# A 2-layer hybrid decoder step: tile products in two PSUM banks, reordered copies, gate work and output pieces, and a VectorE transposition in place of a third product

## The reference

```python
lmat = jnp.where(strict, jnp.einsum('nbhid,nbhjd->nbhij', kb, kc) * decay, 0.0)
rhs = jnp.concatenate([kb * jnp.exp(gc)[..., None], vc * bc[..., None]], axis=-1)
sol = lax.linalg.triangular_solve(eye + lmat, rhs, left_side=True, lower=True, unit_diagonal=True)
...
def step(S, xs):
    v_new = u_i - jnp.einsum('bhck,bhkv->bhcv', w_i, S)
    o = (jnp.einsum('bhck,bhkv->bhcv', q_i * jnp.exp(g_i)[..., None], S)
         + jnp.einsum('bhij,bhjv->bhiv', qk_i, v_new))
    S = S * jnp.exp(g_last)[..., None, None] + jnp.einsum('bhck,bhcv->bhkv', k_dec, v_new)
    return S, o
```

## Time and profile before

| | |
|---|---|
| median of 3 runs | 3659.48 us (3659.13 to 3660.59) |
| the profiled execution | 3668.19 us, its span 3666.5 us |
| PE busy | 3337.3 us, 91% of the span |
| DVE / ACT / POOL busy | 1865.3 / 827.3 / 847.5 us |
| granted TensorE clock, whole span | 0.922 |

### The profile page before, as it was taken

One profiled execution on the slowest core, in us unless ns is written; L12 is line 12 of the kernel. 1 busy time (PEld: TensorE's weight loads), 2 busy tenths in 40 slices (PEclk: granted clock), 3 DMA queues, 4 the chain that ended last, 5 costly groups with the idle time before them and its releaser, 6 DMA issues.

```text
span 3666.5 us, 74612 instructions
## 1 busy us (share of the span) xinstructions
PE 3337.3 (91%) x32699; PEld 3143.0 (86%) x32699; DVE 1865.3 (51%) x4027; ACT 827.3 (23%) x1897; POOL 847.5 (23%) x776
## 2 busy tenths in 40 slices
PE   6889898989898898988999999995699899999998
PEld 5878797978787787877999999994499799999997
DVE  5445555455554454556876777635512433423334
ACT  3334333324242332333010111002200300000001
POOL 2102020202020111201333333332323133333331
PEclk8879898989898897989999999996699899999999
DMA  2111111111111111110112222226611011111111
GB/s 90 55 42 50 59 44 59 47 49 52 48 54 44 55 55 49 48 42 30 49 61 84 72 84 78 71 65 217 180 41 47 29 47 47 47 47 47 47 48 62
DMA packets 111348, 223.82 MB, mean 61 GB/s; under 512 B 24880, under 2 KB 59184, under 8 KB 110000
## 3 DMA queue, kind: packets, MB, share of 16 engines
q1 hardware_dynamic: 82400, 177.66, 15.2%
q10 hardware_dynamic: 28624, 41.38, 3.5%
HBM read 177.86 MB, written 41.14 MB: 60 GB/s over the span
## 4 chain that ended last, share of the span: by engine, by line
PE 85%; DVE 8%; ACT 3%; issue 2%; DMA 2%; SPq 1%; POOL 0%; POOLq 0%; DVEq 0%; ACTq 0%
PE ps L218 31%; PE ps L626 15%; PE ps L1360 14%; PE ps L702 5%; PE ps L660 4%; PE ps L677 1%; PE ps L234 1%; PE ps L671 1%; PE ps L653 1%; PE ps L638 1%; DVE x L1172 1%; PE ps L727 1%; PE ps L789 1%; PE ps L295 1%; DVE dwork L1282 1%
## 5 line engine op out<-in xcount | busy, mean ns | idle before, releaser
L218 PE MATMUL ps<-hhi,whi 128*128 128x344 f32 x2424 | 779.1, 321 | 19.1 <-DVE hlo L1829 15.3
L218 PE MATMUL ps<-hhi,wlo 128*128 128x344 f32 x2424 | 776.3, 320 | 0.0
L218 PE MATMUL ps<-hlo,whi 128*128 128x344 f32 x2424 | 775.6, 320 | 0.0
L2099 POOL TENSOR_TENSOR wtick<-wtick 128x1 f32<-128x1 f32 x213 | 46.5, 218 | 2619.4 <-PE ps L218 811.9
L2102 POOL TENSOR_TENSOR wlo<-wraw,whi 128x1024 fp32r<-128x1024 f32 x213 | 531.1, 2493 | 17.1
L218 PEld LDWEIGHTS ps<-hhi,whi 128*128 128x128 f32 x2424 | 457.6, 189 | 21.8 <-issue 17.0
L218 PEld LDWEIGHTS ps<-hhi,wlo 128*128 128x128 f32 x2424 | 457.3, 189 | 0.0
L218 PEld LDWEIGHTS ps<-hlo,whi 128*128 128x128 f32 x2424 | 456.7, 188 | 0.1
L626 PE MATMUL ps<-hhi,whi 128*128 128x344 f32 x1152 | 395.6, 343 | 5.1 <-DVE olo L1092 2.7
L626 PE MATMUL ps<-hhi,wlo 128*128 128x344 f32 x1152 | 376.2, 327 | 0.0
L626 PE MATMUL ps<-hlo,whi 128*128 128x344 f32 x1152 | 376.1, 326 | 0.0
(11 more groups left out here) (366 smaller groups left out, 5544.1 us busy)
## 6 DMA issues: line engine op xcount, KB each, us to landing
wraw<-in_w SPq DMA_DIRECT2D x213, 512.0 KB, 3.3
dwork<-keep_rows SPq DMA_DIRECT2D x64, 256.0 KB, 3.7
tab<-keep_tab SPq DMA_DIRECT2D x8, 1088.0 KB, 6.4
S<-in_sin ACTq DMA_DIRECT2D x16, 512.0 KB, 3.7
drw<-keep_del SPq DMA_DIRECT2D x32, 256.0 KB, 3.3
out_sout<-S ACTq DMA_DIRECT2D x16, 512.0 KB, 2.8
keep_u<-hs SPq DMA_DIRECT2D x8, 580.0 KB, 3.2
uu<-keep_u SPq DMA_DIRECT2D x8, 580.0 KB, 7.7
```

What stands on the lines that cost most here:

```text
L218: ins = nc.tensor.matmul(out, w, r[:, kt, blk(n)], start=k == 0, stop=k == 3 * KT - 1)
L2099: G.tensor_tensor(wtick[:, 1:2], wtick[:, 0:1], wtick[:, 0:1], ALU.add)
```

## The change

- `LEV` goes: P products of all four matrices go to bank `LP` = 0 (columns 32j), T and Y to bank `LT` = 1. The tile order is now j outside, zone inside: four consecutive tile matmuls have four zones and one bank. Banks 2 and 3 join `aside` in the level stage (`free`).
- The T product of levels 1 to 4 goes. DVE adds Y alone (L1291) and then transposes the sum in 32x32 blocks into the T half (L1293). T5 stays on PE.
- The copy `NTc` moves from ACT to DVE (L1136), behind NT. `T5` moves from DVE to ACT (L915). `YD` is done after `Y5` (zones 2, 3) and after P6 (zones 0, 1), not ahead of it. P6 waits for `T5` alone; `vn` waits for `YD` also.
- `gate_mul` moves from slot 5 to 7, `gate_lo` from 7 to 10, `gate_hi` from 6 to 9. In the next i's first projection the gate sum moves behind the fourth half block, and its ACT and DVE parts behind those of the chain.
- Output pieces move to other slots (quad 0: 7 to 6; quad 1: 2, 7 to 5, 9; quad 2: 7, 8 to 6, 9; quad 3: 7 to 5).

```diff
@@ -556,16 +556,18 @@
         SLOTS = 12
-        COL_P, COL_T, COL_Y = 0, Z, 2 * Z
         DENSE = (0, 1, 2, 3, 5, 6, 7)
-        LEV, CB = (0, 1, 2, 3), 4
+        LP, LT, CB = 0, 1, 4
...
-        def across(col, w, r=slice(0, P)):
-            return ps[r, 0:4, col:col + w]
-        PIECE_SLOTS = ((0, 1, 2, 3, 4, 7, 8, 9), (0, 2, 3, 4, 6, 7), (0, 3, 4, 7, 8), (0, 3, 4, 6, 7))
+        def of_p(r=slice(0, P)):
+            return ps[r, LP, 0:4 * Z].rearrange("p (j n) -> p j n", n=Z)
+
+        def of_ty(r=slice(0, P)):
+            return ps[r, LT, 0:8 * Z].rearrange("p (j n) -> p j n", n=2 * Z)
+        PIECE_SLOTS = ((0, 1, 2, 3, 4, 6, 8, 9), (0, 3, 4, 5, 6, 9), (0, 3, 4, 6, 9), (0, 3, 4, 5, 6))
...
@@ -593,8 +595,8 @@
             held = {}
-            dense = 0
-            free = {5: 0, 6: 0, 7: 0}
+            dense = base = 0
+            free = {2: 0, 3: 0, 5: 0, 6: 0, 7: 0}
...
@@ -606,7 +608,10 @@
                 dense += 1
-                return use(DENSE[(dense - 1) % 7], who, name)
+                b = DENSE[(dense - 1) % 7]
+                if b in free:
+                    free[b] = base + dense / 100
+                return use(b, who, name)
...
@@ -653,12 +658,21 @@
-            def tiles(col, lhsT, rhs):
-                for d in range(4):
-                    for j in range(4):
-                        r = zone((j + d) % 4)
-                        ins = nc.tensor.matmul(ps[r, LEV[j], col:col + Z], lhsT(r, j), rhs(r, j), start=True, stop=True)
+            def tiles(out, lhsT, rhs):
+                for j in range(4):
+                    for z in range(4):
+                        r = zone(z)
+                        ins = nc.tensor.matmul(out(r, j), lhsT(r, j), rhs(r, j), start=True, stop=True)
                 return ins
+
+            def to_p(r, j):
+                return ps[r, LP, Z * j:Z * j + Z]
+
+            def to_t(r, j):
+                return ps[r, LT, 2 * Z * j:2 * Z * j + Z]
+
+            def to_y(r, j):
+                return ps[r, LT, 2 * Z * j + Z:2 * Z * j + 2 * Z]
...
@@ -672,6 +686,7 @@
                     p.after("DVE", g + "Y6")
+                    p.after("ACT", g + "YD")
...
@@ -757,30 +772,26 @@
                     for h in range(2):
-                        jj = (j + h) % 4
                         up, low = zone(2 * h), zone(2 * h + 1)
-                        ins = nc.tensor.matmul(ps[low, LEV[jj], COL_P:COL_P + Z], DEC[q % 2][up, jj, low], W[up, jj, 0:Z], start=True, stop=True)
+                        ins = nc.tensor.matmul(to_p(low, j), DEC[q % 2][up, j, low], W[up, j, 0:Z], start=True, stop=True)
...
                 for j in range(4):
-                    ins = nc.tensor.matmul(ps[zone(1), LEV[j], COL_T:COL_T + Z], W[zone(1), j, Z:2 * Z], PP[zone(1), j], start=True, stop=True)
-                p.go(ins, gq + "T5")
+                    ins = nc.tensor.matmul(to_t(zone(1), j), W[zone(1), j, Z:2 * Z], PP[zone(1), j], start=True, stop=True)
...
                     for h in range(2):
-                        jj = (j + h) % 4
                         up, low = zone(2 * h), zone(2 * h + 1)
-                        ins = nc.tensor.matmul(ps[up, LEV[jj], COL_Y:COL_Y + Z], PP[low, jj], W[low, jj, Z:2 * Z], start=True, stop=True)
+                        ins = nc.tensor.matmul(to_y(up, j), PP[low, j], W[low, j, Z:2 * Z], start=True, stop=True)
...
                 slot(i, q, 10)
-                p.after("DVE", gq + "T5")
-                p.after("ACT", gq + "Y5")
+                p.after("ACT", gq + "T5")
                 for j in range(4):
-                    ins = nc.tensor.matmul(ps[H:P, LEV[0], j * H:(j + 1) * H], DEC[q % 2][0:H, j, H:P], TOP[0:H, j], start=True, stop=True)
+                    ins = nc.tensor.matmul(ps[H:P, LP, j * H:(j + 1) * H], DEC[q % 2][0:H, j, H:P], TOP[0:H, j], start=True, stop=True)
...
@@ -797,20 +808,20 @@
                     p.after("DVE", gq + f"TY{l - 1}")
-                    p.go(tiles(COL_P, lambda r, j: NM[r, l - 1, j], lambda r, j: W[r, j, 0:Z]), gq + f"P{l}")
+                    p.go(tiles(to_p, lambda r, j: NM[r, l - 1, j], lambda r, j: W[r, j, 0:Z]), gq + f"P{l}")
...
                     p.after("ACT", gq + f"P{l}")
-                    tiles(COL_T, lambda r, j: W[r, j, Z:2 * Z], lambda r, j: PP[r, j])
-                    p.go(tiles(COL_Y, lambda r, j: PP[r, j], lambda r, j: W[r, j, Z:2 * Z]), gq + f"PY{l}")
+                    p.go(tiles(to_y, lambda r, j: PP[r, j], lambda r, j: W[r, j, Z:2 * Z]), gq + f"PY{l}")
...
                 e = i - 1
+                dense, base = (0 if i else 2), i * NQ * SLOTS - 1
...
                         chain(e, NQ - 1, k)
-                        if k == 0:
+                        if k == 3:
...
@@ -826,14 +837,15 @@
                 gram(i, 0, take)
+                free[DENSE[(dense - 1) % 7]] = base + 2
...
                     pass
-                for b in LEV:
+                for b in (LP, LT):
...
                     levels(i, q)
-                for b in LEV:
-                    held[b] = ("ACT", f"{i}.{NQ - 1}.P6")
+                held[LP] = ("ACT", f"{i}.{NQ - 1}.P6")
+                held[LT] = ("ACT", f"{i}.{NQ - 1}.Y5")
...
@@ -887,28 +899,22 @@
-            def diagonal(i, q):
-                g = f"{i}.{q}."
-                a.after("DVE", g + "NT")
-                for z in range(1, 4):
-                    a.go(A.activation(DEC[q % 2][zone(z), :, 0:Z], DEC[q % 2][zone(z), :, zone(z)], AF.Copy), g + "NTc")
-
...
-            def spread_y(i, q):
-                g = f"{i}.{q}."
-                for z in range(4):
-                    a.go(A.activation(YY[q % 2][zone(z), :, zone(z)], TY[q % 2][zone(z), :, Z:2 * Z], AF.Copy), g + "YD")
-
-            def fifth_y(i, q):
+            def spread_y(i, q, zones):
+                for z in zones:
+                    a.go(A.activation(YY[q % 2][zone(z), :, zone(z)], TY[q % 2][zone(z), :, Z:2 * Z], AF.Copy), f"{i}.{q}.YD")
+
+            def fifth(i, q):
...
                 a.after("PE", g + "PY5")
-                for z in (0, 2):
-                    a.go(A.activation(YY[q % 2][zone(z), :, zone(z + 1)], across(COL_Y, Z, zone(z)), AF.Copy), g + "Y5")
+                a.go(A.activation(TOP[zone(1), :, 0:Z], of_ty(zone(1))[:, :, 0:Z], AF.Copy), g + "T5")
+                for z in (2, 0):
+                    a.go(A.activation(YY[q % 2][zone(z), :, zone(z + 1)], of_ty(zone(z))[:, :, Z:2 * Z], AF.Copy), g + "Y5")
...
@@ -937,8 +943,6 @@
                     decay(i, q + 1)
-                if s == 6 and q >= 2:
-                    gate_hi(f"{i}.{q - 2}.", gate_cols(q - 2), f"{i - 1}.out{KT - 1}.{q - 2}" if i else None)
...
@@ -975,8 +979,10 @@
                 if i:
+                    for k in (1, 2):
+                        chain(e, NQ - 1, k)
                     gate_r(f"{e}.{NQ - 2}.", QCH * CH)
-                    for k in (1, 2, 5, 6):
+                    for k in (5, 6):
...
@@ -1017,9 +1021,10 @@
                                 a.after("PE", gq + f"PY{l - 1}")
-                            a.go(A.activation(PP, across(COL_P, Z), AF.Copy), gq + f"P{l}")
+                            a.go(A.activation(PP, of_p(), AF.Copy), gq + f"P{l}")
                         else:
-                            a.go(A.activation(PP6[H:P], ps[H:P, LEV[0], 0:4 * H].rearrange("p (j n) -> p j n", n=H), AF.Copy), gq + "P6")
+                            a.go(A.activation(PP6[H:P], ps[H:P, LP, 0:4 * H].rearrange("p (j n) -> p j n", n=H), AF.Copy), gq + "P6")
+                            spread_y(i, q, (0, 1))
...
@@ -1126,11 +1131,14 @@
                     v.go(V.scalar_tensor_tensor(M[:, j], ps[:, b, (2 + j % 2) * P:(3 + j % 2) * P], tg[:, 0, j // 2, c:c + 1], M[:, j], ALU.mult, ALU.mult), g + "NT")
+                v.after("DVE", g + "NT")
+                for z in range(1, 4):
+                    v.go(V.tensor_copy(M[zone(z), :, 0:Z], M[zone(z), :, zone(z)]), g + "NTc")
...
                 W, M = TY[q % 2], DEC[q % 2]
-                v.after("ACT", g + "NTc")
+                v.after("DVE", g + "NTc")
...
@@ -1194,9 +1202,9 @@
                         gate_sq(i, q - 2)
-                    if s == 5:
+                    if s == 7:
                         gate_mul(i, q - 2)
-                    if s == 7:
+                    if s == 10:
...
@@ -1249,9 +1257,10 @@
                     gate_sq(e, NQ - 2)
+                    for k in (3, 4):
+                        chain(e, NQ - 1, k)
                     gate_mul(e, NQ - 2)
-                    for k in (3, 4, 7):
-                        chain(e, NQ - 1, k)
+                    chain(e, NQ - 1, 7)
...
@@ -1279,11 +1288,10 @@
                             v.after("PE", gq + f"PY{l}")
-                            v.go(V.tensor_tensor(W, across(COL_T, 2 * Z), W, ALU.add), gq + f"TY{l}")
-                        elif l == 5:
-                            v.after("PE", gq + "T5")
```

(16 more changed lines are left out.)

## The result

The changed kernel takes 3489.1 us (median of 4 runs, 3480.5 to 3494.8), the kernel before 3660.0 us (4 runs, 3659.1 to 3667.8). The ratio is 0.953 [0.950, 0.955].

A forecast was written before the change was run, and what follows sets the result against it. PE was taken to bound the kernel, busy 91% of the span, losing time to short waits and half clock. Terms summed to -104 us: 3564 us for the profiled execution, 3555 us median; range 3465 to 3660.

The forecast's parts named there:

- T products, -32: Levels on PE: 128 T products gone save 40 us, 8 us return as waits for vn; net -32 us.
- The rival with zones that serialize in one bank: Tile products on PE: four zones sharing a bank would not overlap, costing 240 us; 3795 us, chance 0.12.
- Level chain on DVE, 0: DVE's addition plus transposition makes T some 0.2 us later per level; PE's other work covers it: 0, at worst +26 us.
- P6, -19: Quad ends on PE: 51.4 us of waits before P6 go, 1.0 us before PY6 comes in 32 quads; net -19 us.
- Banks, -30: Output pieces in level stages: with five banks, not three, their 33.8 us of waits for bank readers mostly go; -30 us.
- Gate, -14: Next projection: the gate sum, moved four half blocks on, no longer waits for DVE's square in seven places; -14 us.
- DVE's order, 0: DVE's queue: moving gate_mul removes most of vn's 18.1 us wait, but a new wait after quad 2 cancels it; 0.
- DVE's burst at quad ends, +16: Other quad ends: DVE's burst, about as long as PE's work, adds 0.5 us a quad; +16 us.
- The rival in which DVE takes PE's place: PE waits for DVE's added work and longer quad-end bursts, with no clock gain; middle 3627 us, chance 0.20.
- Clock, -25: PE's half clock behind stalls of 2.5 us or more: some 15 go, worth 45 us, taken as -25 us.
- The rival in which the clock follows: Half-clock stretches behind quads go, -90 in place of -25, with PE's quad-end waits; 3490 us, chance 0.15.

The follow-up runs named there:

- pc_five: Changed kernel with output pieces put back in quad 0 (slot 6 to 7), quad 1 (5 to 2) and quad 3 (5 to 7): 3517.0 us, 0.960.
- stall: Changed kernel with P6 also waiting for the x addition of an output piece on DVE, in 21 places, no work added: 3536.3 us, 0.967.
- u_copies: Changed kernel with copies as before: NTc on ACT, all of YD ahead of Y5, T5 on DVE, P6 behind Y5: 3520.8 us, 0.962.
- p6_early: Changed kernel with ACT copying P6 out before the second Y5 and vb, so that PY6 need not wait: 3455.2 us, 0.944.

## Why the forecast had the sign and most steps right, and the size too small

**T products, -32: too large.** Put back, they are 37 us of work, near the 40 of the prediction. But 16 us of idle time go with them, not 8, and some clock. Measured +10 when undone.

**The rival with zones that serialize in one bank: refuted.** In the trace after, 211 of the 247 unbroken groups of level products are 32 rows that take 0.45 us in one bank, as they did in four; 27 more take 0.65, as 25 did before. The Trainium skill (TensorEngine Tiling (Array Packing), Restrictions and Gotchas) says that row tiles cannot access the same bank simultaneously; where each zone writes its own partitions of the bank, this trace shows no cost, and the measurement decides. The rival's price of 0.4 us and more a product did not appear.

**Level chain on DVE, 0: right.** L665 waits 4.2 us for the transposition where it waited 8.1 for the addition; with 4.2 at L698 and 2.2 at L776 it is some 2 us more in all. The dependent pair takes 0.64 us, from 859.53 to 860.17, close to the 0.29 + 0.30 of the earlier trace rows.

**P6, -19: right in mechanism.** The predicted new wait of 1.0 us x 32 = 32 was measured as 31 waits, 32.3 us; the old 51.4 fell to 6.6, not to 0. Undone it is worth 32, all of it idle time, for P6 then waits 80 us and not 51.

**Banks, -30: right.** The waits went as said; 24 when done alone or undone.

**Gate, -14, and DVE's order, 0.** The gate sum gained 12.4, vn 12.2, against a new 6.5 for qg (L1153) and 2.6 for S. I had let the new wait cancel the gain of vn; it took half. Undone together 14, within the scatter of both.

**DVE's burst at quad ends, +16: too large.** The waits for qg (6.5) and S (2.6) are new, 9 us in all, and X's fell. The rival in which DVE takes PE's place failed by this: DVE's busy share of the stretch rose from 52 to 62% and it waited for PE at the end of quad 1 all the same (0.71 before L1296).

**Output piece slots: no term.** I priced their banks but not their place. It is the largest single part, 46 us; 28 are lost when `pc_five` puts some of the pieces back. The release of GpSimd's split by the last piece is a chain through three engines (GpSimd, DVE, ACT) that I did not follow.

**Clock, -25: the step that failed in size.** The prediction gave each of some 15 stalls 3 us, took 45 us, and cut this to 25, "but half clock also stands behind stretches with no stall". Measured are -85 between the profiled executions, some 60 to 70 in the mean. The cut was wrong, and so is the working behind it: a price per long stall. `stall` shows some 20 us of clock for 21 stalls, net of the shorter waits that they replace: 1 us each and not 3. `u_copies` brings 21 gaps of 2 us and more back at no clock loss, `p6_early` takes waits of 1 us away and 21 us of loss go, and the T products put back lower it by 18. The count missed the short waits: P6 waited 25 times before (10 + 9 + 6) and the pieces 27 times, most of them for less than 2.5 us, while I took 15 stalls. What in the pattern of work and waits sets the clock, and which of the five parts gave how much of it, is not shown.

The rival in which the clock follows gave 3490 us, and 3489 was measured. This is luck in part: its -90 of clock is 20 to 30 too many, its work 10 too many, and the idle time fell by 36 more than the forecast's terms that it kept; the wait that it wanted gone at quad ends stayed (32.3 us at PY6).

**The other idle time.** Of the 36 us of idle time that the forecast lacks, 12 are vn, which it let a new wait cancel, and at least 7 the burst that stayed away. Pieces in other slots had no term; undone, they bring 26 us of idle time back.

The five parts undone singly give 46 + 32 + 24 + 14 + 10 = 126 of the 171 us. By means it is 131 of 172, by ratios 148 of 173, and the error of the part that is missing is some 30 us. So 25 to 45 us are not assigned to one part, and it is not sure that they are more than scatter.

## What to carry to other kernels

Judge the clock by all executions, not by two profiled ones: four executions of the changed kernel differ by 25 us in their clock loss, as much as any single part moved it. Waits of PE cost more than their length here, the long ones and those of 1 us, where half clock follows them; `stall` cost 47 us for 28 us of idle time, and taking the 1 us waits away gave 34 for 20. But `u_copies` cost 32 for 32, so this is no fixed price. When an engine's wait is long though its releaser is short, follow the releaser's own queue back through each engine, down to GpSimd, and look at what a moved instruction sets free. Taking work off PE was worth little where the next product then waits for another engine's result: 37 us of products gave 10.
